# Attention scores on TensorE: two maps alternated by half of the keys, under one wait

## The reference, cut to what matters

```python
def diff_attention(q, k, v, lam):
    ...
    scale = DQK_B ** -0.5            # DQK_B = 64
    def one_block(qblk):             # 128 queries
        s = jnp.einsum('bqhmd,bkhmd->bhmqk', qblk, k).astype(jnp.float32) * scale
        p = jax.nn.softmax(s, axis=-1)
        a = p[:, :, 0] - lam * p[:, :, 1]
        return jnp.einsum('bhqk,bkhe->bqhe', a.astype(v.dtype), v)
```

## Time and profile before

| | |
|---|---|
| median of 3 runs | 1556.33 us |
| lowest, highest | 1556.08, 1559.58 us |
| profiled execution | 1557.05 us |
| its span, first to last instruction | 1555.2 us |
| TensorE busy | 1477.3 us (95%) |
| VectorE busy | 1043.3 us (67%) |
| ScalarE busy | 601.4 us (39%) |
| mean granted TensorE clock | 0.975 |

### The profile page before, as it was taken

One profiled execution on the slowest core, in us unless ns is written; L12 is line 12 of the kernel. 1 busy time (PEld: TensorE's weight loads), 2 busy tenths in 40 slices (PEclk: granted clock), 3 DMA queues, 4 the chain that ended last, 5 costly groups with the idle time before them and its releaser, 6 DMA issues.

```text
span 1555.2 us, 29812 instructions
## 1 busy us (share of the span) xinstructions
PE 1477.3 (95%) x11798; PEld 1373.2 (88%) x11798; DVE 1043.3 (67%) x1943; ACT 601.4 (39%) x1180; POOL 154.1 (10%) x148
## 2 busy tenths in 40 slices
PE   6899999999999999999997878899999999999998
PEld 2799999999999999987785667899999999998886
DVE  4977777787365757553877887678887777753333
ACT  4522222221123533443556434354544444444223
POOL 0000000000000000020003545764000000000000
PEclk9999999999999999999996878999999999999999
DMA  9345444545244312211102100012123222221222
GB/s 341 102 144 151 142 152 149 154 143 161 82 149 136 96 46 77 59 55 42 42 2 62 43 30 16 22 53 71 55 59 91 81 81 86 81 77 69 81 68 95
DMA packets 174582, 141.85 MB, mean 91 GB/s; under 512 B 8464, under 2 KB 156437, under 8 KB 173461
## 3 DMA queue, kind: packets, MB, share of 16 engines
q1 hardware_dynamic: 151652, 117.89, 24.4%
q10 hardware_dynamic: 22833, 22.59, 4.6%
HBM read 137.01 MB, written 3.45 MB: 90 GB/s over the span
## 4 chain that ended last, share of the span: by engine, by line
PE 83%; DVE 10%; issue 3%; ACT 2%; SPq 1%; DMA 1%; POOL 0%; DVEq 0%; ACTq 0%
PE ps L2326 15%; PE ps L2328 14%; PE ps L2327 14%; PE ps L2478 5%; PE ps L2476 5%; PE ps L2477 5%; PE ps L2548 3%; PE ps L2547 3%; PE ps L2546 3%; PE ps L2756 1%; PE ps L2879 1%; PE ps L2909 1%; PE ps L2777 1%; PE ps L2923 1%; PE ps L3001 1%
## 5 line engine op out<-in xcount | busy, mean ns | idle before, releaser
L2326 PE MATMUL ps<-h_hi,w_lo 128*128 128x320 f32 x1152 | 364.7, 317 | 11.7 <-DVE h_lo L1429 4.5
L2328 PE MATMUL ps<-h_hi,w_hi 128*128 128x320 f32 x1152 | 356.9, 310 | 0.0
L2327 PE MATMUL ps<-h_lo,w_hi 128*128 128x320 f32 x1152 | 356.9, 310 | 0.0
L1382 DVE TENSOR_TENSOR w_lo<-w_raw,w_hi 128x1024 fp32r<-128x1024 f32 x120 | 147.7, 1233 | 228.9 <-ACT w_hi L748 228.6
L2326 PEld LDWEIGHTS ps<-h_hi,w_lo 128*128 128x128 f32 x1152 | 217.4, 189 | 18.5 <-DVE h_lo L1429 7.2
L2327 PEld LDWEIGHTS ps<-h_lo,w_hi 128*128 128x128 f32 x1152 | 217.6, 189 | 0.8 <-issue 0.2
L2328 PEld LDWEIGHTS ps<-h_hi,w_hi 128*128 128x128 f32 x1152 | 217.2, 189 | 0.0
L748 ACT CAST w_hi<-w_raw 128x1024 fp32r<-128x1024 f32 x120 | 125.6, 1048 | 197.3 <-PE ps L2328 107.8
L1516 DVE SCALAR_TENSOR_TENSOR ada_acc<-ada_ffn,cond,ada_acc 128x256 f32<-128x256 f32 x392 | 161.7, 478 | 1.2
L2326 PE MATMUL ps<-act_hi,w_lo 128*128 128x320 f32 (+1 forms) x352 | 108.9, 309 | 2.1 <-DVE mods L1545 2.1
L2328 PE MATMUL ps<-act_hi,w_hi 128*128 128x320 f32 (+1 forms) x352 | 108.5, 308 | 0.0
(11 more groups left out here) (413 smaller groups left out, 3015.8 us busy)
## 6 DMA issues: line engine op xcount, KB each, us to landing
w_raw<-in_w_ffn_in SPq DMA_DIRECT2D x64, 512.0 KB, 3.8
w_raw<-in_w_ffn_out SPq DMA_DIRECT2D x44, 512.0 KB, 3.8
ada_ffn<-in_w_ada ACTq DMA_DIRECT2D x43, 512.0 KB, 4.0
w_raw<-in_w_in SPq DMA_DIRECT2D x28, 512.0 KB, 3.7
ada_ffn<-in_w_ffn_in SPq DMA_DIRECT2D x20, 512.0 KB, 3.7
ada_k<-in_w_ada SPq DMA_DIRECT2D x8, 1024.0 KB, 11.1
ada_ffn<-in_w_ada SPq DMA_DIRECT2D x13, 512.0 KB, 3.4
w_raw<-in_w_out SPq DMA_DIRECT2D x8, 512.0 KB, 3.3
```

Source lines behind the costliest of these rows:

```text
L1382: nc.vector.tensor_tensor(w_lo[at], w_raw[s][:], w_hi[at].bitcast(F32), ALU.subtract)\
L2326: nc.tensor.matmul(out, lo, xh, start=start, stop=False)
L2327: nc.tensor.matmul(out, hi, xl, start=False, stop=False)
L2328: return nc.tensor.matmul(out, hi, xh, start=False, stop=stop)
```

## The change

`scores(v)` waits once, for both exponentials of the unit before (`s_exp` at 2v), and then issues the products. For 640 keys it goes over the halves of the keys first and over the maps inside, so the four products stand as map 0 and map 1 on the first 320 keys, then map 0 and map 1 on the second 320. Each map's second product still counts `s_mm` up by one. For 128 keys the two products stand as before. Operands, banks, the number of products and all other functions are the same.

```diff
@@ -2744,18 +2744,20 @@
 
             def scores(v):
                 hb, q0, nk = ATT_UNITS[v]
-                for m in range(2):
-                    if v >= 1:
-                        pe.wait_ge(s_exp, 2 * v - 1 + m)
-                    rows = slice(m * DK, m * DK + DK)
-                    q = q_b[rows, hb, q0:q0 + P]
-                    if nk == P:
-                        ins = nc.tensor.matmul(ps[:, 2 * m, 0:P], q, k_b[rows, hb, 0:P], start=True, stop=True)
-                    else:
-                        for half in range(2):
-                            ins = nc.tensor.matmul(ps[:, 2 * m + half, 0:HT], q, k_all[rows, hb, half * HT:half * HT + HT],
+                if v >= 1:
+                    pe.wait_ge(s_exp, 2 * v)
+                rows = [slice(m * DK, m * DK + DK) for m in range(2)]
+                q = [q_b[x, hb, q0:q0 + P] for x in rows]
+                if nk == P:
+                    for m in range(2):
+                        nc.tensor.matmul(ps[:, 2 * m, 0:P], q[m], k_b[rows[m], hb, 0:P], start=True, stop=True).then_inc(s_mm, 1)
+                else:
+                    for half in range(2):
+                        for m in range(2):
+                            ins = nc.tensor.matmul(ps[:, 2 * m + half, 0:HT], q[m], k_all[rows[m], hb, half * HT:half * HT + HT],
                                                    start=True, stop=True)
-                    ins.then_inc(s_mm, 1)
+                            if half == 1:
+                                ins.then_inc(s_mm, 1)
 
             def turn(v):
                 nk = ATT_UNITS[v][2]
```

## The result

| | median | lowest | ratio to before, 95% interval |
|---|---|---|---|
| before, 20 runs | 1558.94 us | 1556.08 us | |
| changed, 20 runs | 1563.4 us | 1559.33 us | 1.0025 (1.0014 to 1.0035) |

The changed kernel is slower by 0.25%, some 4 us. The forecast had no change that can be told (within 0.3%) and a small loss of 1.8 us. It is a loss, and within 0.3%. The time does not hold: 1563.4 lies above the range, which ended at 1562.0. Two things are to be explained, a start level that was too low, and a loss that is over twice the forecast one.

The account below looks back on a forecast made before the run. A race of TensorE and VectorE bounds each attention unit. Alternation 0 plus wait 1.8 us took the profiled 1557.05 to 1558.9, so the median to 1558.1 us; range 1555.5 to 1562.0.

Parts of the forecast that it names:

- start level: Whole kernel: profiled execution 1557.05 us lies 0.7 above the median 1556.33, so 1558.9 there means a median of 1558.1.
- The products overlap already: Score units on TensorE: both maps' passes already run in pairs, 1.35 us per unit instead of 2.4 in line.
- lagging unit 10: Attention unit where map 1 waits for its exponential; map 1's lag of 0.92 us was to delay map 0 too.
- Alternation costs 0: Part 1, 16 units of 640 keys: order m0, m1, m0, m1 leaves unlagged units at 1.35 us, cost 0.
- The wait costs 1.8 us on VectorE's path: Part 2, attention stage: map 0 now waits for the later exponential, delaying VectorE's reductions; TensorE leaves 1.8 us late.
- V: Lateness of VectorE's first reduction in a unit, carried through the stage: 0.35 us at unit 4, 1.80 at unit 18.
- the 0.5 us left to it: ScalarE's other work in the stage: idle time covers the difference; if not, the sum grows by 0.5 us.
- rival C: No cost: the next stage absorbs the delay, or map 1 was not waiting for ScalarE; 1556.3 us, 10%.
- The clock term: Whole kernel: the sum has no clock cost; only rival D allows for shifted clock falls.
- rival D: Behind the attention stage: a 1.8 us shift moves where the granted clock falls and rises; 1555 to 1562 us, 13%.

Follow-up runs that it names:

- one row half: Kernel before with both maps computed from the rows of map 0, leaving out map 1's scores; ratio 1.0063, median 1570.03 us.
- Order only: Changed kernel's product order m0, m1, m0, m1 with the two separate waits of the kernel before; ratio 0.9999, stage 101.2 us.
- changed twice: The changed kernel measured against the kernel before, then once more unaltered; ratios 1.0025 and 1.0009.
- wait only: Kernel before with its old product order but the change's single wait for both exponentials; ratio 1.0008, stage 99.0 us.
- large units: Kernel before with the single wait in the 16 units of 640 keys alone; ratio 1.0022, stage 99.0 us.
- small-units kernel: Kernel before with the single wait in the four units of 128 keys alone; ratio 0.9994, stage 101.2 us.
- the filled kernel before again: Repeat of the kernel before with 12 extra unread products at the attention stage's opening; ratio 0.9984, median 1557.37 us.
- the changed one with its opening filled: Changed kernel with 12 extra unread products at the attention stage's opening; ratio 1.0016 to the kernel before, stage 99.0 us.
- The kernel before with its opening filled: Kernel before plus 12 unread products in TensorE's idle time at the attention stage's opening; first ratio 0.9994, median 1557.91 us.

## Why the prediction was right or wrong

- **The products overlap already:** right, shown by the single file of 2.42 us in one row half. The Trainium skill's rule of strict program order ("TensorE: Matmul & The Clock Gate", Part 3, The mechanism) does not hold for two row halves here: map 1's first pass started beside map 0's first, past three passes written ahead of it. One number of the prediction is off: with starts in written order map 1 would begin as late as in the lagging unit 10, and a unit would take some 2.26 us, not 2.4.
- **Alternation costs 0:** right. Order only is at 0.9999 with units of 1.35 and 2.26 us.
- **The wait costs 1.8 us on VectorE's path:** right in mechanism and size, for the stage. In the executions without a fall the stage is 98.9 to 99.0 against 97.1, and V agrees within 0.03 us in eight units. ScalarE asked for none of the 0.5 us left to it, and the next stage covered nothing in the four unfilled kernels with this wait in the large units (739.6 to 740.4 us behind the stage, 739.5 before), so rival C is out.
- **The start level was wrong.** The step is "that execution lies 0.7 above the median 1556.33, so the median goes to 1558.1". Three runs gave a median near the floor of a wide distribution; 20 gave 1558.94. This is 2.6 us of the 5.3 by which 1563.4 misses 1558.1.
- **The clock term was mis-sized.** The sum holds nothing for the clock, and rival D looked behind the stage only, because there the trace had its 0.51. In the stage it read 1.00, and I took that for safe. The runs showed 4.0 us for a fall at the opening and 1.4 for one at unit 10, in some executions; and behind the stage D was not wrong, since that part took 738.1 to 743.5 us. With 4.5 us between the medians, 1.8 of the wait leave 2.7, which is what 1563.4 misses beyond the start level. The four measurements of the single wait in the large units without fill (changed twice, wait only, large units) average 1.0016, 2.5 us, which leaves 0.7, within the noise of four intervals that reach 1.6 to 2.2 us to either side. So part of the 2.7 was probably luck of the first measurement (1.0025, and 1.0009 for the same kernel again), and whether the wait causes any of the rest is not shown: the opening fell in order only and in the small-units kernel too, and in none of the three other executions with this wait in the large units.
- **The range** took its upper end from three runs that spread by 3.5 us. The 20 runs of before spread by 8.3 and went up to 1564.36, so 1562.0 was too low an end for any kernel that is a little slower.

What stays open: why the same idle time brings a fall in one execution and none in the next. The place of the stage in time differs by 2 us between executions (first scores at 717.9 to 720.1); this was not controlled. Most of it goes with one thing: the three executions whose stage began at 719.5 to 720.1 (order only, the filled kernel before again, the changed one with its opening filled) had one more stretch at 0.50 long before it; the nine others, at 717.9 to 718.5, had not. In the filled kernel before again it reads:

```profile
362.90:366.30 3.40, 3.40 (x14) 3.40 (x14) 3.37 (x7) 1.62 (x2) 0.00 (x0) 0.50 0.60 165
```

Open as well is what makes the part behind the stage differ by up to 5.4 us. The three executions of unfilled kernels whose stage ends 1.8 us later without a fall took 0.8 to 0.9 us more there than the kernel before, with the granted clock at 0.79 instead of 0.81 between 820 and 1010 us; but the filled kernels before, whose stage is 97.1 us, took 1.7 and 4.0 more, so it can't be put down to the wait.

The kernel before with its opening filled has the lowest ratios, 0.9994 and 0.9984, a gain of 0.06% and 0.16%, and only the second is clear of 1.

## What to carry to other kernels

Before reordering products to make them overlap, look at the starts of the records: here two row halves of the array ran side by side in either written order. A wait is another matter: it holds all that is written behind it, the other map's product too. When two waits are merged into one, the cost is on the engine that used the earlier result, and it can be worked out unit by unit from that engine's idle time. A median of three runs is no level to put a forecast on when the effect is a tenth of a per cent.

## What the runs showed of the hardware

- A pass of a 64-row f32 product with 320 columns takes 0.27 us, as long as one of 128 rows; two of them in different row halves take 0.27 together.
- The first pass of one row half started some 0.02 us behind the first of the other half, past three passes written ahead of it (unit 8 of the kernel before, 1.35 us for eight passes). In one row half the same products queue, 2.42 us. In the lagging unit 10 map 1 starts 0.92 us after map 0, when map 0 has started its last pass, and the unit takes 2.26.
- The opening of the stage, with TensorE busy 1.63 of 3.50 and 1.40 of 3.40 us in two of them, was followed by some 10 us at 1.2 GHz in three executions; with 1.69 of 3.50 it was not. Each cost 4.0 us (17.7 against 21.7 from the first scores to unit 4's reduction, wait aside). Twelve unread products in the idle time cost nothing, and none of the four executions with them had the fall, against three of eight without.
- Runs of one unchanged kernel spread from 1556.08 to 1564.36 us, and in the profiled executions the same second half of the program took 738.1 to 743.5 us.
